# Turned tiles one chunk later, two output blocks side by side, and conditioning rows that end earlier in the feed-forward

## The reference

```python
def first_block(x, c, ...):
    h = rms_norm(x, norm1_w) * (1.0 + scale1) + shift1
    u_pool, q, k, v, g_a, g_b = split(h @ w_in)
    y_a = multiscale_pool(u_pool, w_pool, pool_scale) @ w_a_up
    y_b = stick_breaking_attention(rms_norm(q), rms_norm(k), v) @ w_b_up
    merged = sigmoid(g_a) * y_a + sigmoid(g_b) * y_b
    x = x + gate1 * (merged @ w_o)
    h2 = rms_norm(x, norm2_w) * (1.0 + scale2) + shift2
    return x + gate2 * (square(relu(h2 @ w_ff1)) @ w_ff2)

def second_block(x, c, positions, ...):
    aq, ak, av, gq, gf, gi, gg = split((rms_norm(x) * (1.0 + scale1) + shift1) @ w_in)
    attn = rms_norm(dilated_attention(rope(rms_norm(aq)), rope(rms_norm(ak)), av))
    hg = rms_norm(hgrn2(gq, gf, gi, lb)) * silu(gg)      # the recurrence
    x = x + gate1 * (concatenate([attn, hg]) @ w_out)
    h2 = rms_norm(x, norm2_w) * (1.0 + scale2) + shift2
    return x + gate2 * (square(relu(h2 @ w_ff1)) @ w_ff2)
```

## Time and profile before

| what | us |
|---|---|
| median of 3 runs | 2602.59 (2600.03 to 2607.41) |
| the profiled execution | 2602.57 |
| its span | 2600.8 |
| PE busy | 2521.6 (97%) |
| DVE busy | 2015.3 (77%) |
| ACT busy | 1277.8 (49%) |
| POOL busy | 272.3 (10%) |
| read from HBM | 659.39 MB, 254 GB/s over the span |

### The profile page before, as it was taken

How to read it: one execution, slowest core, us unless ns; L and a number is a source line. 1 busy time by engine, 2 the same in 40 slices (tenths; PEclk the granted TensorE clock), 3 DMA queues, 4 the chain that set the end, 5 groups by cost and what they waited for, 6 DMA issues and landing times.

```text
span 2600.8 us, 32612 instructions
## 1 busy us (share of the span) xinstructions
PE 2521.6 (97%) x12429; PEld 2112.8 (81%) x12429; DVE 2015.3 (77%) x2305; ACT 1277.8 (49%) x1657; POOL 272.3 (10%) x321
## 2 busy tenths in 40 slices
PE   6999999999999999999999999999999999999998
PEld 5877787878888888888877878887888888888887
DVE  6778879998978888898887798885766666665566
ACT  4544454434555445544445554465455544554453
POOL 1000120202030202002020001350000000020000
PEclk9999999999999999999999999999999999999999
DMA  9998869897989889897966765464567677766654
GB/s 350 334 344 316 286 196 352 322 330 251 324 279 322 316 305 333 274 354 261 330 206 223 233 199 182 146 217 154 186 210 229 224 227 231 230 211 193 189 189 149
DMA packets 298364, 663.66 MB, mean 255 GB/s; under 512 B 20752, under 2 KB 21104, under 8 KB 297184
## 3 DMA queue, kind: packets, MB, share of 16 engines
q1 hardware_dynamic: 294976, 650.21, 74.2%
q0 software_dynamic: 2656, 9.66, 1.1%
q10 hardware_dynamic: 576, 1.70, 0.2%
HBM read 659.39 MB, written 2.10 MB: 254 GB/s over the span
## 4 chain that ended last, share of the span: by engine, by line
PE 81%; DVE 9%; DMA 3%; issue 3%; ACT 3%; POOL 0%; SPq 0%; DVEq 0%; ACTq 0%
PE PS L638 80%; DVE WL L1509 3%; DVE ACC L1517 2%; ACT WH L1095 2%; DVE UQ L1509 1%; DMA RAW<-in_w_o 1%; DMA RAWX<-in_w_in 1%; PE PS L641 1%; DMA RAW<-in_w_in 0%; DMA RAWX<-in_w_o 0%; DMA RAW<-in_w_ada 0%; DVE acc L1509 0%; DVE hn L1517 0%; DVE AL L1509 0%; DMA RAW<-in_w_ff 0%
## 5 line engine op out<-in xcount | busy, mean ns | idle before, releaser
L1095 ACT ACTIVATE WH<-RAW 128x1024 fp32r<-128x1024 f32 x567 | 600.3, 1059 | 782.4 <-PE PS L638 609.9
L1509 DVE TENSOR_TENSOR WL<-RAW,WH 128x1024 fp32r<-128x1024 f32 x567 | 703.9, 1242 | 356.3 <-ACT WH L1095 355.7
L638 PE MATMUL PS<-WH,AH 128*128 128x512 f32 x2052 | 812.0, 396 | 17.8 <-DVE WL L1509 12.1
L638 PE MATMUL PS<-WH,AL 128*128 128x512 f32 x2052 | 800.4, 390 | 0.0
L638 PE MATMUL PS<-WL,AH 128*128 128x512 f32 x2052 | 799.9, 390 | 0.0
L638 PE MATMUL PS<-HL,WH 128*128 128x512 f32 x2048 | 723.8, 398 | 6.3 <-DVE HL L1517 5.1
L638 PE MATMUL PS<-HL,WL 128*128 128x256 f32 x2048 | 574.9, 281 | 0.0
L638 PEld LDWEIGHTS PS<-WH,AH 128*128 128x128 f32 x2052 | 386.1, 188 | 105.8 <-DVE WL L1509 22.1
L638 PEld LDWEIGHTS PS<-HL,WH 128*128 128x128 f32 x2048 | 384.6, 188 | 102.7 <-issue 9.0
L638 PEld LDWEIGHTS PS<-WH,AL 128*128 128x128 f32 x2052 | 385.6, 188 | 81.9
L638 PEld LDWEIGHTS PS<-WL,AH 128*128 128x128 f32 x2052 | 386.3, 188 | 76.8 <-issue 0.2
(11 more groups left out here) (251 smaller groups left out, 1968.9 us busy)
## 6 DMA issues: line engine op xcount, KB each, us to landing
RAW<-in_w_ff SPq DMA_DIRECT2D x335, 512.0 KB, 4.0
RAW<-in_w_ada SPq DMA_DIRECT2D x284, 512.0 KB, 5.1
RAW<-in_w_in SPq DMA_DIRECT2D x192, 512.0 KB, 4.5
RAWX<-in_w_ada SPq DMA_DIRECT2D x100, 512.0 KB, 5.3
RAWY<-in_w_ff SPq DMA_DIRECT2D x96, 512.0 KB, 4.1
RAWX<-in_w_ff SPq DMA_DIRECT2D x81, 512.0 KB, 5.2
RAWX<-in_w_in SPq DMA_DIRECT2D x48, 512.0 KB, 5.4
RAW<-in_w_out SPq DMA_DIRECT2D x32, 512.0 KB, 3.6
```

The costliest lines, as they stand in the source:

```text
L638: return e.matmul(o, l, r, start=start, stop=stop, skip_group_check=True)
L1095: return e.activation(o, i, f, **kw)
L1509: return e.tensor_tensor(o, a, b, op)
```

## The change

Three edits, with what they need:

- The merged tiles are turned from chunk 151 on instead of 150, on PE, ACT and DVE alike. In the same way every group's four pieces (`ada_made`) are taken up one turn earlier.
- The 16 chunks of oa no longer go block by block: the first eight alternate between blocks 0 and 1 as `OA_ORDER` says. Tiles 4 and 5 are turned after chunk 562 and 6 and 7 after chunk 564. Both halves of block 0 are read in one turn. Blocks 2 and 3 keep their order.
- The five groups of conditioning rows in the first feed-forward are dealt out over its chunks 0 to 222, with 10 empty places between groups, instead of 0 to 240 with 12. No DMA is added or removed.

```diff
--- before.py
+++ after.py
@@ -27,7 +27,7 @@
 POOL0 = 71
 QKN0 = 83
 STK0 = 87
-MIX0 = 150
+MIX0 = 151
 HG0 = 475
 ROPE0 = 514
 DIL0 = 541
@@ -42,6 +42,13 @@
           + [(0, 4, 6), (1, 4, 6)] + [(n, 2, 6) for n in range(2, 6)]
           + [(n, 6, 8) for n in range(6)] + [(n, 2, 8) for n in range(6, 12)] + [(n, 4, 8) for n in range(12, 16)])
 SUMS = (0, 21, 41, 61)
+
+
+OA_ORDER = [(0, 0), (0, 1), (1, 0), (1, 1), (0, 2), (1, 2), (0, 3), (1, 3)] + [(n, c) for n in (2, 3) for c in range(4)]
+OA_FIRST = [OA_ORDER.index((n, 0)) for n in range(4)]
+OA_TICKS = [OA_ORDER.index((n, 3)) + 1 - OA_FIRST[n] for n in range(4)]
+
+TURN_HG = {GM0 + 12: 0, GM0 + 14: 2, OA + 2: 4, OA + 4: 6}
 
 
 def sum_parts(q):
@@ -186,7 +193,7 @@
     head += [c for n in range(4) for c in w(I["w_b_up"][0], 0, 8, n * 512)]
     head += [c for n in range(4) for c in w(I["w_o"][0], 0, 16, n * 512)]
     in2 = [c for n in IN2_ORDER for c in w(I["w_in_2"][0], 0, 16, n * 512)]
-    in2 += [c for n in range(4) for c in w(I["w_out_2"][0], 8, 8, n * 512)]
+    in2 += [w(I["w_out_2"][0], 8 + 2 * c, 2, n * 512)[0] for n, c in OA_ORDER]
     in2 += [c for n in range(4) for c in w(I["w_out_2"][0], 0, 8, n * 512)]
     plan += quarter[0]
     head = spread(head, [ada1[2], ada1[3], ada1[4]], 64, 178)
@@ -196,7 +203,7 @@
             plan.append(head[a + i])
             plan += quarter[q][16 * i // n:16 * (i + 1) // n]
     plan += head[60:]
-    plan += spread(ff(I["w_ff1"][0], I["w_ff2"][0]), [ada1[5], ada2[0], ada2[1], ada2[3], ada2[4]], 0, 240)
+    plan += spread(ff(I["w_ff1"][0], I["w_ff2"][0]), [ada1[5], ada2[0], ada2[1], ada2[3], ada2[4]], 0, 222, 10)
     in2 = spread(in2, [ada2[2][24:]], 96, 116)
     in2 = spread(in2, [ada2[2][6:24]], 30, 66)
     plan += spread(in2, [ada2[2][:6]], 4, 28)
@@ -288,7 +295,7 @@
 
     out += ff("ff", FF)
     out += [("in2", i, IN2 + 8 * i, 8) for i in range(14)]
-    out += [("oa", n, OA + 4 * n, 4) for n in range(4)]
+    out += [("oa", n, OA + OA_FIRST[n], OA_TICKS[n]) for n in range(4)]
     out += [("ob", n, OB + 4 * n, 4) for n in range(4)]
     out += ff("fg", FG)
     return out
@@ -356,7 +363,7 @@
     def both(self, q):
 
         name, n = self.all[q][:2]
-        return (name, n) in (("wo", 3), ("ff2", 31), ("ob", 3), ("fg2", 31)) or (name == "in2" and n >= 12)
+        return (name, n) in (("wo", 3), ("ff2", 31), ("oa", 0), ("ob", 3), ("fg2", 31)) or (name == "in2" and n >= 12)
 
     def ended(self, j):
 
@@ -591,7 +598,7 @@
             if not by_pe:
                 reduced[b, g] = 8 * len(reduced)
             for n in range(4):
-                fin.setdefault(tick + (n if by_pe else 4 + (3 * n + 1) // 2), []).append((b, g, n))
+                fin.setdefault(tick + (n if by_pe else 3 + (3 * n + 1) // 2), []).append((b, g, n))
             if g in (2, 5):
                 gates[b, g] = 4 * len(gates)
             else:
@@ -1007,8 +1014,8 @@
                     hgrn(i, s)
                 for h, s in due(p, DIL0, 8, 2, (0, 2, 6, 8)):
                     dilated(h, s)
-                if p in (GM0 + 12, GM0 + 14, OA + 1, OA + 2):
-                    k = {GM0 + 12: 0, GM0 + 14: 2, OA + 1: 4, OA + 2: 6}[p]
+                if p in TURN_HG:
+                    k = TURN_HG[p]
                     turn_hg(k)
                     turn_hg(k + 1)
                 if OA + 8 <= p < OA + 12:
@@ -1043,8 +1050,10 @@
             for j in range(AUP, NW):
                 if j in starts:
                     q = starts[j]
+                if OA <= j < OA + 16:
+                    q = bl.at["oa", OA_ORDER[j - OA][0]]
                 name, n, at, ticks = bl.all[q]
-                c = j - at
+                c = OA_ORDER[j - OA][1] if name == "oa" else j - at
                 if j in norms:
                     for i in range(4):
                         turn_x(j, i)
```

## The result

| | before | after |
|---|---|---|
| median of the runs, us | 2605.00 (2600.03 to 2607.64, 4 runs) | 2590.71 (2589.32 to 2593.94, 4 runs) |
| profiled execution, us | 2602.57 (span 2600.8) | 2589.60 (span 2587.8) |

The ratio is 0.9946, with a 95% interval of 0.9935 to 0.9958. A second measurement of the same two kernels gave 2590.15 us after and 2605.68 us before, with the ratio 0.9946 again (0.9934 to 0.9959). The forecast was 2589.2 us in a range of 2583 to 2596: the change makes the kernel faster, by about the amount forecast. The forecast started from 2602.6 us, the median of three runs; with the fourth it is 2605.00, and the gain between the medians is 14.3 us, where 13.4 were forecast.

The account below looks back on a forecast made before the run. TensorE, busy 97% of the span, bounds the kernel, so time can only come from where it stands or runs slowly: 0 + 0 + 6.0 + 8.4 - 1.0 = 13.4 us off 2602.6 gives 2589.2 us, range 2583 to 2596.

Parts of the forecast that it names:

- Part 1: Merge before w_o: turning tiles one chunk later gains 0, since DVE is busy; bounds 5.1 us gain, 0.8 loss.
- Part 2: Conditioning pieces finished one turn earlier: no wait arises, since 13.9 us of slack are left; cost 0.
- Part 3: Recurrence's output: first two output blocks side by side gain 6.0 us in idle time and slow clock; bounds 4 and 7.
- Part 4, the tail: Chunks 420 to 439: ending conditioning rows at chunk 222 relieves DVE, gaining 8.4 us; bounds 6.2 and 9.4.
- Part 4, the middle: First feed-forward's middle: four per cent more data may exhaust DMA for moments; 1.0 us lost, bounds 0 and 6.6.
- Rival A: Merge before w_o: PE's waits are worth their 5.1 us, giving 2584 us; chance 8%.
- the residual forecast at 0.6: Recurrence's output: a PE wait of 0.6 us for MLO is left, ahead of chunk 566.
- The clock's 1.4 us: Recurrence's output, chunks 561 to 563: gain from the granted clock no longer falling, worth at most 1.8, taken as 1.4.
- Rival D: Recurrence's output: ACT makes chunks 566 and 568 late, so 3 us of 6 are left, 2592 us; chance 10%.
- the ring's residue of 1.0 us: Tail, from chunk 434: raw tiles have four slots instead of six, making chunks late by 0.5 and another 0.5 us.
- a PE wait inside the groups: Sign against the forecast: PE standing for WL inside the groups of conditioning rows; no PE wait expected in chunks 238 to 412.
- Rivals B and C: Denser groups: B, DMA-bound, loses 6.6 us, 2594.8 us, 18%; C, six-slot ring paces 175 dense chunks, 2629 us, 4%.

Follow-up runs that it names:

- mix_only: Kernel before with only the merged tiles turned a chunk later (`MIX0 = 151`); median 2604.22 us, ratio 1.0001.
- relief150: Kernel before with DVE's share of one group of conditioning rows cut to 64 of 1024 columns, transfers unchanged; 2598.01 us, one run.
- tail_relief: Kernel before with the gate's multiply and add of blocks 24 to 27 cut to 32 of 512 columns; 2599.86 us, one run.
- ring436: Kernel after with the ring of weight pieces going from six sets to four at chunk 436 instead of 434; 2590.72 us, ratio 0.9943.
- ff206: Kernel after with the conditioning rows' end at chunk 206 in place of 222; 2591.70 us, ratio 0.9955.
- best: Kernel after with ring switch at 436, conditioning rows ending at 218, attention's squares split over two turns; 2587.91 us, ratio 0.9931.
- after_again: Kernel after, run once more unchanged; 2590.15 us, ratio to before 0.9946.
- ff_only: Kernel before with only the conditioning rows' end at 222, gaps of 10, and pieces a turn earlier; 2596.20 us, ratio 0.9968.
- relief151: Kernel before with DVE's share of one conditioning group cut to 64 of 1024 columns and `MIX0 = 151`; 2601.85 us, one run.

## Why the prediction was right

By its own steps:

| step | forecast, us | measured, us |
|---|---|---|
| Part 1, turned tiles one chunk later | 0 | 0.7 gained in the two traces; `mix_only` 0.0% (within 0.1%) |
| Part 2, pieces a turn earlier | 0 | no wait names them, but see below |
| Part 3, the output blocks side by side | 6.0 gained | 6.4 gained |
| Part 4, the tail | 8.4 gained | 7.4 gained |
| Part 4, the middle | 1.0 lost | 0.9 lost in one execution, 0.0 in the next |
| sum | 13.4 gained | 13.0 gained by span, 14.3 by the medians |

- **Part 1** held, by its mechanism. The waits for SG went and chunk 178 came 0.06 us later than before (chunk 144 had come 0.75 later, so the stretch itself was 0.7 shorter). It could have failed by DVE not being the pace; `relief150` shows that it is: 31.5 us less of DVE's work gave 7.1 us, and it took the SG waits along with the order unchanged. Rival A (5.1 us) is refuted by `mix_only`.
- **Part 3** held term by term: the 4.84 us of waits went; the residual forecast at 0.6 is 0.53. The clock's 1.4 us can be read by itself, since `mix_only` has the kernel before's code here: its waits are the same to 0.01 us (0.94, 1.08 and 2.82), its clock stayed at 1.00, and the chunks took 30.57 us in place of 32.06. So 1.5 us of the 6.4 are the clock's, and other executions lose none of them or twice as much (last section); the other 4.9 are 4.84 of waits, less the 0.36 left, and by difference 0.4 at the first matmuls behind the waits, as forecast (there put down to weight loads). Rival D (half of the gain) is refuted by 25.64 or 25.65 us in five executions of that code.
- **Part 4, the tail**: the mechanism held (`tail_relief`: DVE's load, not the transfers), and the ring's residue of 1.0 us was 0.84, by the chain that was foreseen and gone in `ring436`. The term was mis-sized by the 1.17 us at chunk 424, less the 0.16 that the ring cost less than forecast. Its cause is in the step on Part 2: "No wait arises" was worked out for the piece's inputs, and rightly; but the piece is itself 1.7 us of DVE's time, and into which DVE turn it falls was left out of the working. It fell into the one with block 24's second half. `ff206` and `best` end the group earlier, and the loss is gone; `ring436`, with the end at 222, has it unchanged.
- **Part 4, the middle**: 0.97 us were lost at chunks 361 to 363. Sums by window and PE's wait, chunks 360 to 367, after:

```profile
1114.26:1136.99 22.73, 22.30 (x97) 17.88 (x96) 20.95 (x19) 9.06 (x9) 5.53 (x3) 1.00 0.99 362
```

```profile
PE PS L645 <- DVE WL L1518: 0.4, 1, 0.4
```

  The DMA share is 0.99 at 362 GB/s. The forecast said that four per cent more "may use up what is left for moments", and that is one such moment. But in `after_again`, `ring436` and `ff_only`, with the same conditioning rows, these chunks take 21.76 us, the yardstick, and chunks 224 to 415 lose nothing. And `tail_relief`, which has the rows of the kernel before, loses 0.92 us at chunks 264 to 266, with a PE wait of 0.5 us for WL. So it is no cost of the denser rows that recurs: either density loses some 0.9 us in one execution and nothing in another. That it depends on how the transfers happen to fall is a guess that nothing here tests. The forecast's 1.0 us is thus met by the one trace and not by its cause. My sentence that a PE wait inside the groups would prove me wrong was too strict.
- **Rivals B and C** (6.6 us, or 28 and more, for denser groups) are refuted by `ff206`, where groups denser still cost 2 us over the same chunks. (C's sum has a slip: (6.7 + 1.1 + 1.2) x 1.901 / 6 is 2.85 us and not 2.86, which would make it 12 us; and the 4 us worked out beside it from 358 GB/s are nearer 5. Neither enters the forecast.) The landings stayed at 5.6 us (page, DMA issues, after), short of the 6.7 from which C decides:

```profile
RAWX<-in_w_ada SPq DMA_DIRECT2D x102, 512.0 KB, 5.6
```

  Of the two statements of the Trainium skill that the prediction weighed, that of "DMA: Bandwidth & Descriptors", section "Where 436 GB/s comes from" (some 358 GB/s for a core's reads) is passed by the 368 GB/s of `relief150` over 41 us; the trace agrees with the Trainium skill's "HBM Reference" (section "Specifications (TRN2)") in so far as a lone core gets more, if only by 3%.

Part of the agreement is luck: 568 to the end gave 1.1 us and 192 to 224 took 1.4, and neither has to do with the change (both are the two paces of the last section). The 0.9 us in the middle, the clock's 1.5 us and the like start of both traces are chances of these executions as well.

## What to carry to other kernels

Where an engine waits for a result of another one that is itself busy without a gap, as at this merge, moving the consumer renames the wait and little more; ask who feeds the late engine, and take load from it or leave the place alone. Interleaving two independent output blocks at the place where fresh operands come from a long path over two other engines took away both waits for them here, and the clock that stands like them cost in five of six executions. When a periodic side job is compressed, look up which turn its last, irregular piece now falls into, and count it as load there, not only as something that has to be ready.

## What the hardware showed that I had not expected

**Two paces of the same code.** The chunks of the first matmul of a feed-forward (8 matmuls of 512 columns and 8 of 256) run at one of two paces, and keep it for some thirty chunks. Groups of PE's instructions by form over chunks 192 to 223, first the kernel after, then `best`:

```profile
L645 PE MATMUL PS<-HL,WH 128*128 128x512 f32 x256 | 91.1, 400 | 4.5 <-DVE HL L1526 4.0 <-issue 0.5
L645 PE MATMUL PS<-HL,WL 128*128 128x256 f32 x256 | 71.9, 281 | 0.0
```

```profile
L645 PE MATMUL PS<-HL,WH 128*128 128x512 f32 x256 | 89.8, 395 | 4.4 <-DVE HL L1525 4.0 <-issue 0.5
L645 PE MATMUL PS<-HL,WL 128*128 128x256 f32 x256 | 71.8, 280 | 0.0
```

The waits are the same, and the granted clock is 1.00 in both. From chunk 199 on the steps are 2.82 to 2.83 us in the one and 2.77 in the other, every one of them, and the stretch takes 97.30 or 95.92 us. The second feed-forward has the same pair (592 to 632: 114.9 or 116.3 us), and it does not follow the first: the kernel after has slow then fast, before and `best` fast then slow, `after_again`, the same program as after, slow then slow. So it can differ between two executions of one program, and is worth 1.4 us each time. A difference of two traces holds up to 2.8 us of it; what chooses is open, and was not tried.

**The clock.** Six executions have the kernel before's code at the recurrence's output, with the same waits of 0.94, 1.08 and 2.82 us. Sums by window, chunks 561 to 563 of `mix_only`, then of `relief150`:

```profile
1775.94:1792.35 16.41, 11.58 (x61) 9.21 (x59) 8.39 (x15) 6.67 (x14) 0.00 (x0) 1.00 0.38 127
1761.96:1781.20 19.24, 14.41 (x61) 11.33 (x59) 8.39 (x15) 6.67 (x14) 0.00 (x0) 0.82 0.32 108
```

| executions | granted clock, 561 to 563 | 560 to 568, us |
|---|---|---|
| `mix_only` | 1.00 | 30.57 |
| before, `ff_only`, `tail_relief` | 0.90 | 32.06, 32.03, 31.96 |
| `relief150`, `relief151` | 0.82 | 33.40, 33.33 |

In the trace before the clock fell behind the wait of 1.08 us (0.79 over chunk 562), in `ff_only` and `tail_relief` chiefly behind that of 2.82 (0.67 and 0.68 over chunk 563), in `relief150` behind both. The same code lost 0, about 1.5 or 2.8 us by it. With the new order of the tiles the clock stayed at 1.00 over these chunks in all seven executions. A clock loss seen in one trace is thus an expectation and not a fixed price: the gain of Part 3 is 4.9 us in waits and what goes with them, and 0 to 2.8 more.
